# Three orders changed and tiles of two last sums given to GpSimd, in a one-core RetNet and RG-LRU decoder step

## What is computed

```python
h = rmsnorm(x, norm_pre_mix) * (1 + sc1) + sh1            # sc, sh, g come from silu(c) @ w_ada
q, k, v, g, xr, gr = split(h @ w_in)
o, s_new = retention(rope(q), rope(k) * DK ** -0.5, v, s_ret)     # 4 heads, chunk by chunk
ret_y = groupnorm(o) * ret_gn_w * silu(g)
hseq = rg_lru(causal_conv(xr), h_rnn)                     # 12 channel tiles, a scan over time
rnn_y = hseq * gelu(gr)
ga, gb = split(sigmoid(h @ w_mgate + b_mgate))
mixed = (ga * (ret_y @ w_br_ret) + gb * (rnn_y @ w_br_rnn)) @ w_out
x = x + g1 * rmsnorm(mixed, norm_post_mix)
h2 = rmsnorm(x, norm_pre_ffn) * (1 + sc2) + sh2
fg, fu = split(h2 @ w_ffn_in)
y = x + g2 * rmsnorm((silu(fg) * fu) @ w_ffn_out, norm_post_ffn)
```

## Time and profile before

| | us |
|---|---|
| median of 3 runs | 1449.13 (1448.87 to 1451.73) |
| the profiled execution | 1449.33 |
| its span in the profile | 1447.5 |
| PE busy in it | 1377.7 (95%) |
| DVE busy | 717.9 (50%) |
| ACT busy | 484.3 (33%) |
| POOL busy | 181.3 (13%) |

### The profile page before, as it was taken

How to read it: one execution, slowest core, us unless ns; L and a number is a source line. 1 busy time by engine, 2 the same in 40 slices (tenths; PEclk the granted TensorE clock), 3 DMA queues, 4 the chain that set the end, 5 groups by cost and what they waited for, 6 DMA issues and landing times.

```text
span 1447.5 us, 23984 instructions
## 1 busy us (share of the span) xinstructions
PE 1377.7 (95%) x10324; PEld 1281.7 (89%) x10324; DVE 717.9 (50%) x998; ACT 484.3 (33%) x683; POOL 181.3 (13%) x284
## 2 busy tenths in 40 slices
PE   6699999899999899999999999999799999999995
PEld 3599999788997798799889879999799999999995
DVE  4349888522242475267437624966743333332225
ACT  4277778312231231232224123336422222212221
POOL 1013222000113212212320322000000000000000
PEclk8899999999999999999999999999899999999998
DMA  8422222475424434434442443243022222222321
GB/s 340 149 70 73 74 88 74 171 283 180 159 81 147 154 103 132 163 97 141 148 166 67 138 159 133 88 162 120 0 73 88 88 88 88 88 83 81 88 87 62
DMA packets 49930, 172.70 MB, mean 119 GB/s; under 512 B 5537, under 2 KB 7713, under 8 KB 49569
## 3 DMA queue, kind: packets, MB, share of 16 engines
q1 hardware_dynamic: 39456, 135.51, 28.1%
q0 software_dynamic: 9216, 33.56, 6.6%
q10 hardware_dynamic: 1152, 2.10, 0.4%
HBM read 149.82 MB, written 21.32 MB: 118 GB/s over the span
## 4 chain that ended last, share of the span: by engine, by line
PE 82%; DVE 9%; ACT 3%; DMA 3%; issue 2%; POOL 0%; SPq 0%; DVEq 0%; ACTq 0%; POOLq 0%
PE ps L760 66%; PE ps L769 3%; PE ps L1005 2%; PE ps L1016 2%; PE ps L808 1%; PE ps L988 1%; PE ps L1048 1%; PE ps L1034 1%; DMA raw<-in_w_brnn 1%; PE ps L891 1%; DMA raw<-in_w_out 1%; DVE w_lo L1517 1%; DMA raw<-in_w_rnn 1%; DVE x_res L1872 1%; DVE rsn L1867 1%
## 5 line engine op out<-in xcount | busy, mean ns | idle before, releaser
L760 PE MATMUL ps<-h_hi,w_hi 128*128 128x272 f32 x2096 | 444.1, 293 | 22.8 <-ACT xs L1287 9.5
L760 PE MATMUL ps<-h_hi,w_lo 128*128 128x272 f32 x2096 | 436.3, 290 | 0.0
L760 PE MATMUL ps<-h_lo,w_hi 128*128 128x272 f32 x2096 | 435.3, 289 | 0.0
L1517 DVE TENSOR_TENSOR w_lo<-raw,w_hi 128x1024 fp32r<-128x1024 f32 (+2 forms) x190 | 226.5, 1195 | 335.3 <-ACT w_hi L1189 332.9
L760 PEld LDWEIGHTS ps<-h_hi,w_hi 128*128 128x128 f32 x2096 | 333.9, 190 | 36.6 <-issue 18.0
L760 PEld LDWEIGHTS ps<-h_lo,w_hi 128*128 128x128 f32 x2096 | 332.4, 190 | 0.0
L760 PEld LDWEIGHTS ps<-h_hi,w_lo 128*128 128x128 f32 x2096 | 330.2, 190 | 0.0
L1189 ACT ACTIVATE w_hi<-raw 128x1024 fp32r<-128x1024 f32 (+2 forms) x190 | 195.6, 1030 | 355.9 <-PE ps L760 241.5
L1791 DVE SCALAR_TENSOR_TENSOR state<-state,ps 128x512 f32<-128x512 f32 x64 | 41.1, 684 | 111.1 <-PE ps L1048 110.9
L760 PE MATMUL ps<-a_hi,w_hi 128*128 128x272 f32 x308 | 63.8, 288 | 2.1 <-DVE a_lo L1526 2.1
L760 PE MATMUL ps<-a_hi,w_lo 128*128 128x272 f32 x308 | 63.8, 288 | 0.0
(11 more groups left out here) (238 smaller groups left out, 1848.8 us busy)
## 6 DMA issues: line engine op xcount, KB each, us to landing
raw<-in_w_head SPq DMA_DIRECT2D x48, 512.0 KB, 3.8
raw<-in_w_fin SPq DMA_DIRECT2D x38, 512.0 KB, 3.4
state<-in_state POOLq DMA_DIRECT2D x32, 512.0 KB, 4.1
out_rs<-state POOLq DMA_DIRECT2D x32, 512.0 KB, 3.9
raw<-in_w_rnn SPq DMA_DIRECT2D x24, 512.0 KB, 3.5
ada_more<-in_w_ada SPq DMA_DIRECT2D x23, 512.0 KB, 6.2
ada_raw<-in_w_ada SPq DMA_DIRECT2D x16, 512.0 KB, 14.6
raw<-in_w_bret SPq DMA_DIRECT2D x16, 512.0 KB, 3.5
```

Source lines behind the costliest of these rows:

```text
L760: mm = nc.tensor.matmul(dst[:, half, :], a, b[:, half * HALF:(half + 1) * HALF], start=first and j == 0, stop=last and j == 2)
L1517: V.tensor_tensor(lo[:, 0:cols], raw_slab(i)[0][:, 0:cols], hi[:, 0:cols].bitcast(F32), ALU.subtract).then_inc(lo_ready, 1)
```

## The change

Four edits, and what they need.

1. **Slabs.** SP issues the loads of the slabs `xr` 1 and `gr` 1 before it waits for `h_ready`, and so ahead of `rg_w` and the three `ada_late` slabs.
2. **Splits.** At n = 11 on DVE the low part of slab `gb` 6 is made behind recurrence 9 and no longer behind 10, and that of `gb` 7 behind recurrence 10 and no longer behind 11.
3. **Keys.** In GpSimd's loop over units the load of unit u+2 moves from the head of the step to its end, behind `k_st` of unit u and the store of unit u-1.
4. **Sums.** GpSimd makes tiles 5, 6, 7 of the second half of x1 and tiles 6, 7 of the second half of y. ACT and SP wait for its signals at these tiles, and SP stores y's tiles of that half in the order 0, 1, 2, 6, 3, 4, 5, 7.

```diff
@@ on SP
                 sp.dma_start(ada_raw[:, n, :], w["w_ada"][n // KD, n % KD]).then_inc(ada_in[n], 16)
+            load_to(pl.slab[("gr", 1, "w", 0)])
             sp.wait_ge(h_ready, KD)
             sp.wait_ge(c4_ready, 1)
             sp.dma_start(rg_w[:], w["w_rg"]).then_inc(rg_in, 16)
...
-            for half in range(2):
-                for k in range(KD):
-                    sp.wait_ge(y_done, KD * half + k + 1)
-                    sp.dma_start(out["y"][:, k, cols_of(half)], xr_[:, k, cols_of(half)]).then_inc(stored, 16)
...
+            own_tiles = [k for k in range(KD) if k not in POOLED_OUT]
+            for i, k in enumerate(own_tiles):
+                sp.wait_ge(y_done, KD + i + 1)
+                store_y(1, k)
+                if i % 3 == 2:
+                    sp.wait_ge(y_pooled, i // 3 + 1)
+                    store_y(1, POOLED_OUT[i // 3])
@@ on ACT, square_of_sum
-                act.wait_ge(x1_ready, KD * half + k + 1)
+                if half and k in POOLED_SUM:
+                    act.wait_ge(x1_pooled, POOLED_SUM.index(k) + 1)
+                else:
+                    act.wait_ge(x1_ready, KD * half + k + 1)
@@ on DVE, the tiles of the RG-LRU
-                for i in recurrences_at(n):
+                gate_slabs = list(GATE_TILES.get(n, ()))
+                last_turns = recurrences_at(n) + (recurrences_at(NR) if n == NR - 1 else ())
+                for i in last_turns:
                     decays(i)
                     recur(i)
-                for m in GATE_TILES.get(n, ()):
+                    if n == NR - 1 and i < NR - 1:
+                        ahead(("gb", gate_slabs.pop(0)))
+                for m in gate_slabs:
                     ahead(("gb", m))
-                    if n == NR - 1 and m == GATE_TILES[n][0]:
-                        for i in recurrences_at(NR):
-                            decays(i)
-                            recur(i)
@@ on DVE, the sums
-            one_over("post", 1)
+            one_over("post", 1, norm_known)
             wait_took(dve, pl.half_tile[("wo", KD - 1, 1)][0])
             samples_normed(gate1)
-            for k in range(KD):
+            for k in range(KD - len(POOLED_SUM)):
                 add_normed(1, k, x1_ready)
-                if k == KD // 2:
-                    product_half(0, 0)
+            product_half(0, 0)
...
-            one_over("post2", 1)
+            one_over("post2", 1, norm_known)
             samples_normed(gate2)
-            for k in range(KD):
+            for k in range(KD - len(POOLED_OUT)):
                 add_normed(1, k, y_done)
@@ on GpSimd
                 for b in range(NB):
                     u = h * NB + b
-                    if STATES <= u + 2 < H * NB:
-                        last = u + 2 - STATES
-                        pool.wait_ge(s_stored[last % STATES], 16 * (last // STATES + 1))
-                        load_state(u + 2)
...
                     if u:
                         store_state(u - 1)
+                    if STATES <= u + 2 < H * NB:
+                        last = u + 2 - STATES
+                        pool.wait_ge(s_stored[last % STATES], 16 * (last // STATES + 1))
+                        load_state(u + 2)
...
+            def add_normed(k, signal):
+                y, x, r = (t[:, HALF:SEQ] for t in (mo[:, k, :], xr_[:, k, :], rsn))
+                do(G.tensor_tensor(y, y, r, ALU.mult))
+                do(G.tensor_tensor(x, x, y, ALU.add), signal, wait=False)
+
+            pool.wait_ge(norm_known, 1)
+            wait_took(pool, pl.half_tile[("wo", KD - 1, 1)][0])
+            for k in POOLED_SUM:
+                add_normed(k, x1_pooled)
+            pool.wait_ge(norm_known, 2)
+            wait_took(pool, ("fo", KD - 1))
+            for k in POOLED_OUT:
+                add_normed(k, y_pooled)
```

More of the change, by code:

```diff
@@ L172, in retention_units @@
     return after
+POOLED_SUM = (5, 6, 7)
+POOLED_OUT = (6, 7)
 NORMALISE_AFTER = [("v", 2), ("v", 3), ("k", 0)]
@@ L538, in hybrid_layer_kernel @@
         a_ready, y_done = sem("a_ready"), sem("y_done")
+        norm_known, x1_pooled, y_pooled = sem("norm_known"), sem("x1_pooled"), sem("y_pooled")
         def vcol(name, i, n=1):
@@ L738, in _, with store_y @@
             load_to(len(pl.slabs) - 1)
-            for half in range(2):
-                for k in range(KD):
-                    sp.wait_ge(y_done, KD * half + k + 1)
-                    sp.dma_start(out["y"][:, k, cols_of(half)], xr_[:, k, cols_of(half)]).then_inc(stored, 16)
+            def store_y(half, k):
+                sp.dma_start(out["y"][:, k, cols_of(half)], xr_[:, k, cols_of(half)]).then_inc(stored, 16)
+            for k in range(KD):
+                sp.wait_ge(y_done, k + 1)
+                store_y(0, k)
+            own_tiles = [k for k in range(KD) if k not in POOLED_OUT]
[5 more added lines that the diff above has]
+                    store_y(1, POOLED_OUT[i // 3])
             sp.wait_ge(stored, 16 * (1 + 2 * KD))
@@ L1862, in add_held, with one_over @@
                 add_to_norm(i + 1, m, cols_of(half), norm_summed if m == KD - 1 else sq_added)
-            def one_over(key, half):
+            def one_over(key, half, signal=None):
                 wait_freed(dve, (key, half))
                 r = rsn[:, cols_of(half)]
-                do(V.reciprocal(r, r))
+                do(V.reciprocal(r, r), signal)
             def add_normed(half, k, signal):
```

## The result

| | before | after |
|---|---|---|
| median | 1449.56 us (1448.87 to 1451.73, 4 runs) | 1471.63 us (1470.67 to 1475.45, 4 runs) |
| span in the profile | 1447.5 | 1469.0 |

The changed kernel takes 1.0155 times as long (95% interval 1.0133 to 1.0176): 22 us more, where 5 less were predicted. Lines of the kernel have moved: PE's L760 is L775 now, L1034 (p0 to p3) is L1049, L826 is L841; DVE's L1871 and L1872 are L1889 and L1890; GpSimd's load and store are L2041 and L2048, its tiles of the sums L2092 and L2093.

A forecast was written before the change was run, and what follows sets the result against it. PE, 82% of the chain and busy 95% of the span, was taken as the bound. Span 1447.5 - 11.3 + 2.0 + 1.7 + 2.2 + 0.8 = 1442.9, as a median 1444.5 us; range 1437 to 1449.5.

The forecast's parts named there:

- Keys: GpSimd's unit loop: -4.2 us at unit 7's gap, +6.0 from late state loads at p1 and p3; written +1.7.
- The last rival: Heads 1 to 3: state loads land 7 us after issue, p1 and p3 wait, slow clock follows; 1462 us; chance 5%.
- Slabs: At `xr` 1: PE's 9.46 us gap and the 1.81 us of slow matmuls behind it go; -11.3 us.
- the list of what would show it: Signs to check; for slabs, PE with no gap between `gr` 0 and `xr` 1, and clock 1.0 there.
- Splits: At `gb` 6 and 7: 5.5 us gained, lost again waiting for `bn` 1's second slab, slow clock behind; +2.0 us.
- rival one: The wait for `bn` 1 does not hold the splits' gain: splits give -5.5, total 1437.0 us; chance 12%.
- Rival two: The moved state loads land in time, without the six waits: 1438.5 us; chance 12%.
- x1: Second half of x1's sum: GpSimd's products delay DVE's sums by 3.0 us, PE stands 2.2 us; +2.2 us.
- y: Kernel's end: two tiles less on DVE -1.5, four GpSimd products +2.0, last stores 0.35 us apart; together +0.8 us.
- the third rival: GpSimd and DVE do not collide in the sums of x1 and y: 1440.3 us; chance 10%.
- The fourth rival: In the sums, each GpSimd product blocks DVE for its whole length, 0.69 us: 1446.4 us; chance 7%.
- too short for the slow clock: At unit 7's product: PE's gap shrinks to 2.1 us, so no slow matmuls follow, worth -1.5 us.

The follow-up runs named there:

- slabs_only: The kernel before with the slabs' edit alone: 1439.79 us, ratio to before 0.9913 to 0.9942.
- no_keys: The changed kernel with the state load put back at the head of GpSimd's step, other edits kept: 1444.69 us, ratio to before 0.9947 to 0.9977.
- slabs_splits: The kernel before with the slabs' and the splits' edits: 1440.32 us, ratio to before 0.9917 to 0.9947.
- queue_splits: The kernel before with slabs, splits, GpSimd's order keys, load, store, and SP filling the ring of modulation slabs in smaller portions: 1430.42 us.

## Why the prediction was wrong

**Keys, predicted +1.7, measured +24.9 alone and +26.9 with the rest.** (+27.9 when each kernel is taken against its own runs of the kernel before, 1449.6 and 1450.5.) This one term is the miss, and the step in it that failed is the landing of the moved loads, with what follows from it. Four things, with the trace of after.

1. *The landing.* "A load lands after 4.1 us at the median, and after 5.5 at worst, next to other transfers ... I take 5.2" for p1, and about 4.6 for p3. Measured in heads 1 to 3: 6.0 to 6.4 at p1 and 6.3 to 6.9 at p3. The spacing was right (p1 wants the load 3.7 to 4.0 us after its issue, 3.9 in the prediction). So the six waits are 15.3 us and not 6.0. The rows of before could show only half of this: there each load goes out when the last store has landed, so none of them had a store ahead of it in its queue, and three had a slab beside them, landing after 4.7 to 5.1. After, the loads for p1 and p3 have both. The edit removes the spacing, and a spread of landings measured under it is no bound for the loads behind it. That a store and a slab "are under way" was in the text, but was priced at 1.1 us at p1, and at 0.5 at p3; by the table above the two together cost 2.2.
2. *The clock.* Gaps of 0.5 to 1.5 us were forecast, so no slow matmuls were counted. The gaps were 2.05 to 2.96, and four of the six (2.36 us and more) had the lower clock behind them (0.50 to 0.57 over the next 6 us), about 3 us each: 12 us.
3. *The price of a spell.* 1.8 us by the earlier trace rows counts the 48 matmuls alone; p1, or p3 and the small products behind it, are slowed as well and add 1.
4. *Head 0, predicted -4.2, measured 0.* Unit 7's product indeed starts without a gap, but only since PE stood 0.9 us at p2 and 2.8 at p3 for its loads, with the clock at 0.60 over the 8.5 us behind it. "In head 0 the same wait of p3 falls inside what is left of the gap" put it inside a gap of 2.1; it was longer than that, and brought the slow matmuls back.

15.3 + 12 + 0 = 27 us, against 26.9 to 27.9. The last rival had the mechanism and the place (loads landing 7 us after issue, waits of 3.1 us, slow clock behind, 1462 in all) and got 5% because "no load in this trace but the first four took over 5.5". Its own time was still 10 us short: it counted three spells of 1.8 us, and kept head 0's gain.

**Slabs, predicted -11.3, measured -10.7** (slabs_only). Right, and PE has no gap there, as it should by the list of what would show it.

**Splits, predicted +2.0 (-1 to +3), measured +0.5.** The mechanism is right: no gap over 1.1 us at `gb` 6 and 7, a gap before `bn` 1's second slab, the lower clock behind it, and with less ahead of that slab in the queue the gain is there. The gap was forecast at 7.5 us and is 4.7, because 2.4 are already idled before `bn` 0. So rival one (the wait does not hold the gain) is out. Rival two (the state loads land in time) is out by the landings above.

**Sums.** x1 forecast +2.2: PE is 1.8 us later at the squares in the trace of after, DVE 2.5 late and not 3.0. y forecast +0.8: in the trace of after DVE ends where it would have, and the end comes 0.4 us later. Together 4.4 us by the two kernels without and with them; in the profiled run of no_keys 1.5 of it are slow matmuls at another place (last section). That the two engines don't collide, the third rival, is out. The fourth rival, DVE blocked for the whole of each product (0.69 us), gives more than was seen: a DVE operation grew by 0.4 to 0.5 us beside products of 0.86 and 0.75 us (the means above).

**Sum of the parts**: -10.7 + 0.5 + 26.9 + 4.4 = +21.1; measured +22.1. The 1 us between them is that between the two sets' runs of the kernel before: with +27.9 for the keys the sum is +22.1.

## What to carry to other kernels

A landing time is a property of what is under way when the transfer is issued, in its own queue and in others, and not of the transfer: before moving a load, list what will be issued within a microsecond of it at its new place, and read the landings of loads that already have such neighbours. If there are none, price it by the bytes. Look too at how long before its use the load is issued, since the 20 us that these loads had in hand before hid every landing seen here, and the 4 that were left hide only the shortest. Where an engine serves both a load that others wait for and a store that nobody waits for, the load goes first, and neither stands behind a wait that the other needs. A gain that ends in a wait for a queued transfer is not lost: look at what stands ahead of that transfer and need not.

## What the runs showed of the hardware

The length of a gap of about 2 us does not tell what the clock does behind it. At one place in the FFN PE waits 2.12 us in before, in after and in no_keys. The clock behind it is 1.00 in the traces of before and after and 0.70 in that of no_keys, where it costs 1.5 us. At the same place PE waits 2.49 us in slabs_splits with 1.00 behind, and 2.47 in queue_splits with 0.70. What decides it is not shown. Before, then the wait in no_keys and the stretch behind it:

```profile
1298.20:1304.00 5.80, 5.80 (x46) 5.80 (x47) 1.06 (x1) 0.00 (x0) 0.00 (x0) 1.00 0.28 79
```

```profile
1290.29 0.52 PE L775 MATMUL ps<-a_hi,w_hi 128*128 128x272 f32 x2 [2.12 <-DVE a_lo L1544]
...
1290.30:1296.00 5.70, 5.70 (x33) 5.70 (x34) 1.06 (x1) 0.00 (x0) 0.00 (x0) 0.70 0.27 82
```

Elsewhere it fell behind 1.71, 1.78, 2.36 and 2.44 us and stayed up behind 1.61, 2.05 and 2.23; behind the gaps of 2.79 to 2.96 in the heads of after it fell each time. The prediction's "too short for the slow clock", drawn from one gap of 2.11 us, was no rule.
